# Output squares summed ahead of the norm's product at stage ends, and the scan's normalisation spread, in a 16-stage transformer kernel

## The reference

```python
def rms_norm(x, g):
    return x * rsqrt(mean(x * x, -1) + 1e-6) * g

for i in range(2):                     # in each of the two blocks
    h = h + 0.5 * rms_norm(swiglu(rms_norm(h, g[0]), w13, w2), g[1])
    h = h + rms_norm(mixer_i(rms_norm(h, g[2])), g[3])
    h = h + 0.5 * rms_norm(swiglu(rms_norm(h, g[4]), w13_, w2_), g[5])
    gate = sigmoid(rms_norm(h, g[6]) @ w_gate)
    h = h + rms_norm(gate * (p[i] @ w_proj), g[7])
# mixers: gMLP, RWKV-7, dilated attention, windowed GQA

def rwkv7_mixer(...):                  # 16 heads of 64
    for t in tokens:
        S = S * w_t + (S @ a_t) b_t^T + v_t k_t^T ; y_t = S @ r_t
    yn = (y - mean_head(y)) * rsqrt(var_head(y) + 64e-5)
    yn = yn * lnx[0] + lnx[1]
    bonus = sum_head(r * k * r_k) * v
    return ((yn + bonus) * g) @ w_out
```

## Time and profile before

| | |
|---|---|
| median of 3 runs | 2353.99 us |
| the runs | 2350.56, 2353.99, 2355.45 us |
| time of the profiled execution | 2350.35 us |
| its span | 2348.6 us |
| PE busy, granted clock | 2251.9 us (96%), 0.984 |
| DVE, ACT, POOL busy | 1471.0, 1156.9, 181.9 us |
| matmuls L504, L505, L506 by `XH`/`XL` | 805.4, 784.3, 784.1 us |

### The profile page before, as it was taken

One profiled execution on the slowest core, in us unless ns is written; L12 is line 12 of the kernel. 1 busy time (PEld: TensorE's weight loads), 2 busy tenths in 40 slices (PEclk: granted clock), 3 DMA queues, 4 the chain that ended last, 5 costly groups with the idle time before them and its releaser, 6 DMA issues.

```text
span 2348.6 us, 33586 instructions
## 1 busy us (share of the span) xinstructions
PE 2251.9 (96%) x13285; PEld 1824.1 (78%) x13285; DVE 1471.0 (63%) x2077; ACT 1156.9 (49%) x1670; POOL 181.9 (8%) x289
## 2 busy tenths in 40 slices
...
GB/s 246 188 189 210 181 181 192 181 180 152 225 189 200 174 136 3 3 160 204 163 193 200 189 187 190 183 91 158 189 186 170 206 180 194 176 13 202 190 175 107
DMA packets 289755, 395.60 MB, mean 168 GB/s; under 512 B 11673, under 2 KB 193249, under 8 KB 289601
## 3 DMA queue, kind: packets, MB, share of 16 engines
...
HBM read 392.37 MB, written 1.05 MB: 168 GB/s over the span
## 4 chain that ended last, share of the span: by engine, by line
PE 78%; DVE 6%; ACT 2%; issue 2%; POOL 1%; DMA 0%; DVEq 0%; POOLq 0%; SPq 0%; ACTq 0%
PE bank L504 23%; PE bank L506 23%; PE bank L505 22%; PE bank L530 1%; DVE wl L800 1%; PE bank L518 1%; ACT wh L616 1%; DVE TMP L842 0%; ACT XH L628 0%; DVE H L862 0%; DVE qPS L1830 0%; PE bank L1404 0%; ACT JUNK L623 0%; PE bank L2471 0%; PE bank L2482 0%
## 5 line engine op out<-in xcount | busy, mean ns | idle before, releaser
L800 DVE TENSOR_TENSOR wl<-raw,wh 128x1024 fp32r<-128x1024 f32 x708 | 860.4, 1225 | 570.7 <-ACT wh L616 570.2
L616 ACT ACTIVATE wh<-raw 128x1024 fp32r<-128x1024 f32 x708 | 744.4, 1058 | 658.5 <-PE bank L506 630.1
L504 PE MATMUL bank<-wh,XH 128*128 128x512 f32 x2000 | 805.4, 403 | 18.5 <-ACT wh L616 6.0
L505 PE MATMUL bank<-wl,XH 128*128 128x512 f32 x2000 | 784.3, 392 | 0.0
L506 PE MATMUL bank<-wh,XL 128*128 128x512 f32 x2000 | 784.1, 392 | 0.0
L504 PEld LDWEIGHTS bank<-wh,XH 128*128 128x128 f32 x2000 | 378.5, 189 | 109.9 <-issue 19.4
L506 PEld LDWEIGHTS bank<-wh,XL 128*128 128x128 f32 x2000 | 378.4, 189 | 82.5
L505 PEld LDWEIGHTS bank<-wl,XH 128*128 128x128 f32 x2000 | 379.3, 190 | 73.3 <-issue 0.5
L504 PE MATMUL bank<-wh,AH 128*128 128x512 f32 x704 | 276.0, 392 | 0.0
L506 PE MATMUL bank<-wh,AL 128*128 128x512 f32 x704 | 274.1, 389 | 0.0
L505 PE MATMUL bank<-wl,AH 128*128 128x512 f32 x704 | 274.0, 389 | 0.0
...
## 6 DMA issues: line engine op xcount, KB each, us to landing
...
```

The costliest lines, as they stand in the source:

```text
L504: pe.e.matmul(o, a, h, start=(k == 0), stop=False)
L505: pe.e.matmul(o, a, l, start=False, stop=False)
L616: act.e.activation(self.wh[j % N_W][:, 0:p.size], self.raw[p.chunk % N_RAW][:, p.at:p.at + p.size], ACT.Copy).then_inc(*self.rounded.up(j))
L800: dve.e.tensor_tensor(self.wl[j % N_W][:, 0:p.size], self.raw[p.chunk % N_RAW][:, p.at:p.at + p.size], self.wh[j % N_W][:, 0:p.size].bitca ...
```

## The change

It has three parts.

- The fold of the squares (L852) becomes a function of its own, `dve_mean`. In `dve_out` and `dve_dil_out` it is called ahead of the weighing of half 1, for each tile; in `dve_ple` behind it, as before.
- In embedding stages the weighing doesn't wait for the square any more.
- In the scan: tile 0 makes its four gram products before both krv, and the PSUM pairs are counted from the one behind that of the product "v"; tile 1's bonus moves from the tail to the place before "seen" 1, and both bonuses get other buffers; the normalisation is cut in steps ("centre", "square", "var", "gain", "scale", "add") that stand further apart, for tile 0 over levels 3 to 5 and the "fin"s of tile 1, for tile 1 with its two halves taking turns; a `leave` moves from "fin" to behind "seen" 3; tile 1's turns go from steps 14 and 15 of "out" to 15 and 19.

```diff
--- before.py
+++ after.py
@@ -838,11 +838,12 @@
 
-        dve.wait_ge(self.squared, "out", n, b, t)
+        if STAGES[n][0] != "ple":
+            dve.wait_ge(self.squared, "out", n, b, t)
         dve.e.tensor_tensor(self.TMP[:, t, b, 512:1024], y, self.bct[g][:, b * 512:(b + 1) * 512],
                             ALU.mult).then_inc(*self.weighed.up(n, b, t))
 
-    def dve_resid(self, dve, n, t):
+    def dve_mean(self, dve, n, t):
 
         ss, sm = self.cols(2 * T, "out", n), self.cols(T, "sm", n)
         pre, factor = self.weight(n)
@@ -851,6 +852,10 @@
         dve.wait_ge(self.squared, "out", n, 1, t)
         dve.e.scalar_tensor_tensor(x, ss[:, T + t:T + t + 1], 1.0 / D / factor ** 2, x, ALU.mult, ALU.add).then_inc(
             *self.msum.up(n, t))
+
+    def dve_resid(self, dve, n, t):
+
+        x = self.cols(T, "sm", n)[:, t:t + 1]
         for b in range(2):
             part = self.H[:, t, b * 512:(b + 1) * 512]
             if n == 0:
@@ -881,6 +886,7 @@
             elif i < first:
                 self.leave(dve, p.j + N_W)
         for t in range(T):
+            self.dve_mean(dve, n, t)
             self.dve_weigh(dve, n, 1, t, self.pair((n, "out", 1))[t])
             self.dve_resid(dve, n, t)
             if t == 0 and self.goes_on(n) and layer.tail == 4:
@@ -1581,14 +1588,16 @@
 
     def dve_dil_out(self, dve, n):
         parts = self.layers[n, "out"].parts
-        for b in range(2):
-            self.dve_weigh(dve, n, b, 0, self.pair((n, "out", b))[0])
+        self.dve_weigh(dve, n, 0, 0, self.pair((n, "out", 0))[0])
+        self.dve_mean(dve, n, 0)
+        self.dve_weigh(dve, n, 1, 0, self.pair((n, "out", 1))[0])
         self.dve_resid(dve, n, 0)
         for p in parts[0:2]:
             self.leave(dve, p.j + N_W)
         self.dve_weigh(dve, n, 0, 1, self.pair((n, "out", 0))[1])
         if self.goes_on(n):
             self.dve_x(dve, n + 1, 0)
+        self.dve_mean(dve, n, 1)
         self.dve_weigh(dve, n, 1, 1, self.pair((n, "out", 1))[1])
         self.dve_resid(dve, n, 1)
         for p in parts[2:3] if self.goes_on(n) else parts[2:]:
@@ -2320,9 +2329,7 @@
 
         steps = []
         steps += [("tt", 0, 0), ("tt", 0, 1)]
-        for o in range(2):
-            steps += [("gram", 0, o), ("krv", 0, o)]
-        steps += [("complete", 0)]
+        steps += [("gram", 0, 0), ("gram", 0, 1), ("krv", 0, 0), ("krv", 0, 1), ("complete", 0)]
         for lv in range(1, 6):
             steps += [("level_a", 0, 0, lv), ("level_a", 0, 1, lv)]
             if lv < 5:
@@ -2334,17 +2341,22 @@
                 steps += [("tt", 1, lv - 4)]
         steps += [("fin", 0, 0), ("gram", 1, 0), ("fin", 0, 1), ("krv", 1, 0), ("state", 0), ("gram", 1, 1), ("krv", 1, 1),
                   ("seen", 1)]
-        side = {1: [("state", 1)], 2: [("yo", 0), ("bonus", 0, 0), ("bonus", 0, 1)],
-                3: [("norm", 0, 0, 0, 3)], 4: [("norm", 0, 0, 3, 6), ("norm", 0, 1, 0, 3)], 5: [("norm", 0, 1, 3, 6)]}
+        steps[-1:-1] = [("bonus", 1, 0), ("bonus", 1, 1)]
+        side = {1: [("state", 1), ("bonus", 0, 0), ("bonus", 0, 1)], 2: [("yo", 0)], 3: [("centre", 0, 0)],
+                4: [("square", 0, 0), ("centre", 0, 1)], 5: [("var", 0, 0), ("square", 0, 1), ("gain", 0, 0)]}
         for lv in range(1, 6):
             steps += [("level_a", 1, 0, lv), ("level_a", 1, 1, lv), ("level_b", 1, 0, lv), ("level_b", 1, 1, lv)]
             steps += side[lv]
-        steps += [("fin", 1, 0), ("fin", 1, 1), ("seen", 2), ("turn", 0, 0), ("turn", 0, 1), ("state", 2)]
+        steps += [("fin", 1, 0), ("var", 0, 1), ("gain", 0, 1), ("fin", 1, 1), ("scale", 0, 0), ("add", 0, 0),
+                  ("scale", 0, 1), ("add", 0, 1), ("seen", 2), ("turn", 0, 0), ("turn", 0, 1), ("state", 2)]
         return steps
 
 
-    SCAN_TAIL = (("seen", 3), ("bonus", 1, 0), ("bonus", 1, 1), ("yo", 1), ("norm", 1, 0, 0, 6), ("norm", 1, 1, 0, 6),
-                 ("turn", 1, 0), ("turn", 1, 1))
+    SCAN_TAIL = (("seen", 3), ("part", 6), ("yo", 1), ("centre", 1, 0), ("square", 1, 0), ("centre", 1, 1), ("var", 1, 0),
+                 ("square", 1, 1), ("gain", 1, 0), ("var", 1, 1), ("gain", 1, 1), ("scale", 1, 0), ("add", 1, 0),
+                 ("scale", 1, 1), ("add", 1, 1), ("turn", 1, 0), ("turn", 1, 1))
+
+    SCAN_BESIDE = {2: ("seen", 3), 6: ("yo", 1), 15: ("turn", 1, 0), 19: ("turn", 1, 1)}
 
     def scan_pair(self, pe, key, *until):
 
@@ -2364,14 +2376,14 @@
         return slice(hd * HD, hd * HD + HD)
 
     def pe_rwkv_scan(self, pe, n):
+        self.n_scan = self.place["pair", (n, "v", 1)] + 1
         for step in self.scan_steps():
             self.pe_scan(pe, *step)
-        beside = {2: 0, 6: 3, 14: 6, 15: 7}
         self.n_pairs = 0
 
         def during(step):
-            if step in beside:
-                self.pe_scan(pe, *self.SCAN_TAIL[beside[step]])
+            if step in self.SCAN_BESIDE:
+                self.pe_scan(pe, *self.SCAN_BESIDE[step])
             self.pe_turn_next(pe, n, "out", step)
 
         self.linear(pe, n, "out", self.XH, self.XL, lambda k, t: [(self.moved, "ro", t, k // 4), (self.made, "ro", t, k // 4)],
...
@@ -2652,9 +2664,8 @@
                     "tt", t, o, 1).rearrange("p (i r n) -> p i r n", i=2, r=4)).then_inc(*self.made.up("tt", t, o))
                 if (t, o) == (0, 0):
                     self.leave(dve, self.layers[n, "out"].parts[5].j)
-            elif kind == "fin":
-                if tuple(a) == (1, 0):
-                    self.leave(dve, self.layers[n, "out"].parts[6].j)
+            elif kind == "part":
+                self.leave(dve, self.layers[n, "out"].parts[a[0]].j)
             elif kind == "gram":
                 self.dve_scan_gram(dve, *a)
             elif kind == "level_a":
...
@@ -2758,9 +2767,9 @@
 
     def scan_bonus(self, t):
 
-        return self.AA if t == 0 else self.TB
-
-    def dve_scan_norm(self, dve, t, h, seg):
+        return self.AA[:, 0, :] if t == 0 else self.KK[:, 0, :]
+
+    def dve_scan_norm(self, dve, kind, t, h):
         c = slice(h * 512, (h + 1) * 512)
 
         def wide(x):
@@ -2768,23 +2777,22 @@
 
         x, sq, at = self.R[:, t, c], self.K[:, t, c], 16 * t + 8 * h
         mean, var = self.rSM[:, 128 + at:136 + at], self.rSM[:, 160 + at:168 + at]
-        if seg == 0:
+        if kind == "centre":
             dve.wait_ge(self.moved, "yo", t, h)
             dve.e.tensor_reduce(mean, self.per_head(x), AX, ALU.add).then_inc(*self.made.up("ysum", t, h))
             dve.wait_ge(self.made, "ysum", t, h)
             dve.e.tensor_scalar(mean, mean, 1.0 / HD, None, ALU.mult).then_inc(*self.made.up("ymean", t, h))
-        elif seg == 1:
             dve.wait_ge(self.made, "ymean", t, h)
             dve.e.tensor_tensor(self.per_head(x), self.per_head(x), wide(mean), ALU.subtract).then_inc(
                 *self.made.up("centred_y", t, h))
-        elif seg == 2:
+        elif kind == "gain":
             dve.wait_ge(self.figured, "gl", t, h)
             dve.wait_ge(self.moved, "sq", t, h)
             dve.e.tensor_tensor(x, x, self.GG[:, t, c], ALU.mult).then_inc(*self.made.up("yg", t, h))
-        elif seg == 3:
+        elif kind == "var":
             dve.wait_ge(self.moved, "sq", t, h)
             dve.e.tensor_reduce(var, self.per_head(sq), AX, ALU.add).then_inc(*self.made.up("var", t, h))
-        elif seg == 4:
+        elif kind == "scale":
             dve.wait_ge(self.rs, "gn", t, h)
             dve.wait_ge(self.made, "yg", t, h)
             dve.e.tensor_tensor(self.per_head(x), self.per_head(x), wide(var), ALU.mult).then_inc(
@@ -2792,7 +2800,7 @@
         else:
             dve.wait_ge(self.made, "yn", t, h)
             dve.wait_ge(self.figured, "bonusg", t, h)
-            dve.e.tensor_tensor(x, x, self.scan_bonus(t)[:, t, c], ALU.add).then_inc(*self.made.up("yd", t, h))
+            dve.e.tensor_tensor(x, x, self.scan_bonus(t)[:, c], ALU.add).then_inc(*self.made.up("yd", t, h))
 
     def pool_rwkv_scan(self, pool):
         pool.wait_ge(self.d_one["masks"])
@@ -2809,11 +2817,11 @@
             elif kind == "bonus":
                 t, h = a
                 c, at = slice(h * 512, (h + 1) * 512), 64 + 16 * t + 8 * h
-                bn, gg = self.scan_bonus(t)[:, t, c], self.GG[:, t, c]
+                bn, gg = self.scan_bonus(t)[:, c], self.GG[:, t, c]
                 if t == 0:
                     pool.wait_ge(self.product, "u", 1, 1)
                 else:
-                    pool.wait_ge(self.product, "yo", 0)
+                    pool.wait_ge(self.product, "bt", 0, 1)
                 pool.wait_ge(self.made, "sums", t, h)
                 pool.e.tensor_tensor(self.per_head(bn), self.per_head(self.VV[:, t, c]), self.rSM[:, at:at + 8].unsqueeze(
                     2).broadcast_to([P, 8, HD]), ALU.mult).then_inc(*self.figured.up("bonus", t, h))
@@ -2826,8 +2834,8 @@
                 pool.wait_ge(self.d_one["lnx0"])
                 pool.wait_ge(self.figured, "bonusg", t, h)
```

(4 more changed lines are left out.)

10 lines of the change are left out of this document (4 added, 6 removed).

## The result

| | before | changed |
|---|---|---|
| median | 2353.64 us (4 runs) | 2329.88 us (4 runs) |
| range of the runs | 2350.56 to 2355.45 | 2329.15 to 2331.77 |
| profiled execution, span | 2350.35, 2348.6 | 2330.51, 2328.7 |

The ratio is 0.9902, 95% interval [0.9887, 0.9918]: the change takes off 23.8 us (2353.64 - 2329.88). The forecast was 2326.5 in a range of 2319 to 2339, faster: direction and range hold, and the time was 3.4 us above the forecast. The sum's parts did not all hold, and the two that failed most lie next to each other, at the end of the scan.

A forecast was written before the change was run, and what follows sets the result against it. PE is busy 96% of the span, leaving its waits and lower-clock stretches: 4.3 + 5.8 + 1.95 + 1.6 + 13.8 (scan, less 3 for clock) = 27.45 off 2350.35; plus 3.64 for the median, 2326.5, range 2319 to 2339.

The forecast's parts named there:

- embedding stages, no wait: Embedding stages' ends and the kernel's end: the fold comes forward 0.61 at seven places, 4.3 us gained.
- fold ahead, tile 1 and embeddings: Other ends: tile 1's adds come earlier at six step-7 boundaries and four before embedding stages, 0.58 each, 5.8 us.
- tile 0's waits: Other ends, tile 0's adds: 0.6 each behind rwkv and dilated, 0.1 at five others, 0.25 into rwkv; 1.95 us.
- clock behind dilated: Behind dilated: with the wait cut to 2.15, full clock in place of 0.56 for 3.6 us; 1.6 us.
- scan's start: Start of the scan: wait of 1.41 before the turns gone, half of krv's 3.27 gone; 2.9 us.
- levels 4 and 5: Scan, tile 1: each level costs level 3's time plus 0.2, as tile 0's normalisation steps are spread; 7.0 us.
- to the first product: Scan, up to the first product of "out": DVE's scale step and leave no longer run beside POOL's bonus; 2.2 us.
- tail: Scan's tail: with halves by turns and later turn steps, PE's waits of 7.89 shrink; 4.7 us gained.
- clock, taken off: Scan: 3 us deducted because a denser scan may still enter "out" at half clock.
- The first: Rival, scan's tail: both turns late at their new steps, scan gains 6 to 7, about 2334 to 2338; chance 0.08.
- The hoist: Rival, stage ends: something else ends PE's wait, so 5.8 and 1.95 fall away, 2334; chance 0.05.
- The slower rival: Scan: many short waits keep PE at 1.2 GHz from level 4 through "out", up to 46 more, 2369.5; chance 0.02.

The follow-up runs named there:

- e4: Kernel before, only that the weighing in embedding stages doesn't wait for the square: 2346.12 us, ratio 0.9971.
- again: Second trace of the unaltered changed kernel, taken in run e10: 2329.75 us, ratio 0.9896.
- e6: Changed kernel, only that in the tail the split of tile 1's half 0 goes ahead of half 1's scale and add: 2328.06 us, ratio 0.9889.
- e5: Changed kernel with tile 1's normalisation order (one half, then the other) and turns at steps 14 and 15 put back: 2330.41 us, ratio 0.9902.
- e7: Changed kernel with tile 0's half 0 variance in level 5 and the state's steps ahead of the last scale: 2322.57 us, ratio 0.9858.
- e10: Changed kernel as it is, run again for a second trace: 2329.75 us, ratio 0.9896.
- e9: Changed kernel with tile 1's bonus back in the tail, on its new buffer: 2332.77 us against 2329.75 of the changed kernel on the same chip.

## Why the prediction was right, and where its sum was not

| term | sum | measured, from the traces |
|---|---|---|
| embedding stages, no wait | 4.3 | 4.4 (e4) |
| fold ahead, tile 1 and embeddings | 5.8 | 2.1 at six turns of step 7, 2.5 in four embedding stages |
| tile 0's waits | 1.95 | into rwkv 0.5, behind rwkv 0.5, behind dilated 0.5; elsewhere nothing |
| clock behind dilated | 1.6 | 1.5 |
| scan's start | 2.9 | 3.2 |
| levels 4 and 5 | 7.0 | 7.4 |
| to the first product | 2.2 | -1.3 (again), of which 2.3 is clock; 1.0 at full clock (e6) |
| tail | 4.7 | 0.3 (again) to 1.0 (e5) as a stretch, 1.0 to 1.2 behind "yo" |
| clock, taken off | -3 | no term of its own; in the two lines above |

The measured column, with -1.3 and 0.3 for the two lines at the scan's end, makes 21.6. The span of the changed kernel's second trace is 21.3 shorter than that of the kernel before (2348.6 - 2327.3).

- **What bounds it, and the ends: right, with one price too high.** At the ends of embedding stages each wait moved by what its chain gave up. Behind dilated PE's wait fell by 0.5 and the granted clock stayed full: from tile 0's turns to tile 1's 2.0 were gained there. The slip is at step 7: the 0.62 of the earlier trace rows is the wait of a weight load, and from it I took 0.58 a boundary. The load's wait did go (3.3 in all six), but PE's products had waited 0.22 there, and between the two turns they came 0.28 to 0.40 nearer, 2.1 in all. Tile 0 at the other five ends gave nothing where I had 0.1 each: PE did not wait there.
- **Start of the scan: right in size.** The wait of 1.41 went whole, as I took it, and the stretch gained 1.6. Of krv's 3.27 I took half; a wait of 1.35 is left in the changed kernel, and the stretch gained 1.6.
- **Levels: right.** 7.57 for both, against the 7.8 of "level 3 plus 0.2" for each. The reason was read a little too wide: six steps in a row stood behind level 4 alone, three behind levels 3 and 5.
- **"To the first product": the step that failed first.** The bonus's own effect was right (1.8 measured, 2.2 said). The sentence that scale and add of tile 0 land behind the "fin"s "where PE has both to do" was wrong: PE had its products done 5.2 us after the first "fin" (973.7), and DVE's last add ended at 976.6. I counted the steps out of the levels and not into the place where they went. That cost at least 0.8 by the order, and 3.1 with the clock that fell there; e7, which takes the steps out of PE's way, gave 2.8 at full clock.
- **Tail: mis-sized from a wrong read of the steps.** The length of the chain was right: from ACT's evacuation at 994.08 to the end of the last add it took 11.1, where I said 10.7. The first turn's wait was 1.95 against 2.2 said. For the second turn I had seen that its step uses it at once, and put 1.0 (it is 1.50). What I missed is that step 15 uses the first turn in the same way, and that the low part of half 0 is queued behind the scale of half 1: I had nothing for it, and it is 3.10 (2.74 in e10). Behind that wait six matmuls were 0.43 apart, not 0.23, which is 1.2 more; but the kernel before had some five such behind its 5.69, so little of this counts against it.
- **Luck in the number.** The terms for the first product and the tail were 7.9 too high together (3.5 and 4.4), the fold's 1.2. The 3 us that I took off for clock covered a part of it. They were taken for a fall that did come: from "fin" to PE's first product behind "yo" the same code took 26.8 us in e10 and 22.5 in e6, 4.3 apart. They were not taken for the waits that I had missed, and the range was wide enough for both.
- **The rivals.** The first, the tail takes back what the levels give, is in fact what the two terms at the scan's end did in part. The hoist was not hidden as a whole, and no step changed places for nothing. The slower rival's mechanism did show in one trace (half clock for levels 2 to 4 of tile 0, 7.25 us), but it neither lasted nor came back, and 35 us at half were never near.
- **The bonus's place.** The Trainium skill's page "SBUF — State Buffer", section "Who interferes with whom", says that a DVE instruction with two SBUF inputs contends with a GpSimd instruction that reads SBUF, and that one with at most one SBUF input, outside the two-port modes, doesn't. The traces agree with both. At the old place DVE's two-input steps took 1.52 and 1.63 (e9). At the new one DVE works on a PSUM bank and one SBUF tile: its steps from 938.63 to 939.82 took 0.67 to 0.68 beside the bonus, as in the kernel before without it, and from the first "fin" of tile 0 to level 1 of tile 1 both kernels took 14.12. So nothing was paid there.
